# Attention maps of four chunks or fewer: one bank and one copy for prefix and whole chunks, with two PSUM banks in turn

## What is computed

```python
def block(args):                       # y_a and y_b: one block of 128 queries
    s = jnp.einsum('bqhd,bkhd->bhqk', qi, k).astype(jnp.float32) * scale
    ...                                # y_a adds log_cum[t] - log_cum[s]
    s = jnp.where(mask, s, NEG)        # causal, pad keys never seen
    p = jax.nn.softmax(s, axis=-1)
    return jnp.einsum('bhqk,bkhd->bqhd', p.astype(v.dtype), v)
...
p = jax.nn.softmax(jnp.concatenate([s, sink], axis=-1), axis=-1)[..., :-1]   # y_c
o = jnp.einsum('bnhgqk,bnkhd->bnqhgd', p.astype(v.dtype), vx)
...
branches = jnp.stack([y_a * silu(a_z), y_b * silu(b_z), y_c * silu(c_z)], axis=2)
merged = jnp.sum(sigmoid(gates) * einsum('blnw,nwd->blnd', branches, w_branch), axis=2)
return x + merged @ w_out
```

## Time and profile before

| what | value |
|---|---|
| median of 3 runs | 2737.91 us (2735.36 to 2740.32) |
| the profiled execution's own time | 2737.13 us |
| its span, first to last instruction | 2735.3 us |
| TensorE matmul (PE) busy | 2637.4 us, 96% |
| VectorE (DVE) busy | 1639.7 us, 60% |
| ScalarE (ACT) busy | 1136.1 us, 42% |

### The profile page before, as it was taken

How to read it: one execution, slowest core, us unless ns; L and a number is a source line. 1 busy time by engine, 2 the same in 40 slices (tenths; PEclk the granted TensorE clock), 3 DMA queues, 4 the chain that set the end, 5 groups by cost and what they waited for, 6 DMA issues and landing times. The chain is left out here.

```text
span 2735.3 us, 40191 instructions
## 1 busy us (share of the span) xinstructions
PE 2637.4 (96%) x15248; PEld 2188.7 (80%) x15248; DVE 1639.7 (60%) x3832; ACT 1136.1 (42%) x2518; POOL 129.5 (5%) x140
## 2 busy tenths in 40 slices
PE   8999999999999999999999899999998899999999
PEld 7879889899988777777877577888885658788887
DVE  5475666765547576675678663444567864533346
ACT  4345332543334543443435543333355664432333
POOL 1001000000100100000013000000004300000000
PEclk9999999999999999999999999999998999999999
DMA  4201212222220212222322122232321102323322
GB/s 136 79 30 55 67 42 84 58 74 89 86 80 27 76 58 59 81 66 93 99 81 62 32 89 93 95 98 93 94 90 46 42 1 78 91 95 95 98 96 97
DMA packets 115265, 205.30 MB, mean 75 GB/s; under 512 B 13824, under 2 KB 23680, under 8 KB 114944
## 3 DMA queue, kind: packets, MB, share of 16 engines
q1 hardware_dynamic: 114064, 200.14, 23.8%
q10 hardware_dynamic: 1008, 2.59, 0.3%
HBM read 200.51 MB, written 2.10 MB: 74 GB/s over the span
## 5 line engine op out<-in xcount | busy, mean ns | idle before, releaser
L1879 DVE TENSOR_TENSOR wl<-raw,wh 128x512 fp32r<-128x512 f32 (+2 forms) x738 | 481.3, 677 | 383.8 <-ACT wh L1678 374.4
L1678 ACT ACTIVATE wh<-raw 128x512 fp32r<-128x512 f32 (+2 forms) x774 | 450.6, 605 | 327.0 <-PE pp L2395 239.7
L2389 PE MATMUL pp<-Hh,wh 128*128 128x264 f32 (+1 forms) x2144 | 514.7, 355 | 11.1 <-ACT wh L1678 5.1
L2392 PE MATMUL pp<-Hl,wh 128*128 128x264 f32 (+1 forms) x2144 | 501.1, 348 | 0.0
L2395 PE MATMUL pp<-Hh,wl 128*128 128x264 f32 (+1 forms) x2144 | 499.6, 347 | 0.0
L2389 PEld LDWEIGHTS pp<-Hh,wh 128*128 128x128 f32 x2144 | 354.8, 190 | 71.4 <-issue 11.1
L2392 PEld LDWEIGHTS pp<-Hl,wh 128*128 128x128 f32 x2144 | 358.5, 190 | 51.7 <-issue 5.5
L2395 PEld LDWEIGHTS pp<-Hh,wl 128*128 128x128 f32 x2144 | 357.0, 190 | 51.3 <-issue 4.2
L2389 PE MATMUL pp<-Yh,wh 128*128 128x512 f32 (+1 forms) x1190 | 295.6, 364 | 1.9 <-ACT M L1743 0.7
L2392 PE MATMUL pp<-Yl,wh 128*128 128x512 f32 (+1 forms) x1190 | 289.6, 359 | 0.1
L2395 PE MATMUL pp<-Yh,wl 128*128 128x512 f32 (+1 forms) x1190 | 289.4, 359 | 0.1
(11 more groups left out here) (301 smaller groups left out, 3140.2 us busy)
## 6 DMA issues: line engine op xcount, KB each, us to landing
raw<-in_w SPq DMA_DIRECT2D x698, 256.0 KB, 2.6
raw<-in_w SPq DMA_DIRECT2D x36, 192.0 KB, 2.4
raw<-in_w SPq DMA_DIRECT2D x40, 128.0 KB, 2.0
out<-X SPq DMA_DIRECT2D x8, 256.0 KB, 2.0
con<-in_con SPq DMA_DIRECT2D x1, 1513.0 KB, 7.5
X<-in_x SPq DMA_DIRECT2D x2, 528.0 KB, 5.7
X<-in_x ACTq DMA_DIRECT2D x2, 528.0 KB, 6.6
Z<-in_p ACTq DMA_DIRECT2D x2, 512.0 KB, 3.6
```

What stands on the lines that cost most here:

```text
L1678: e.activation(part("wh", j), landing(j), AF.Copy).then_inc(*act.up("split", j))
L1879: e.tensor_tensor(part("wl", j), landing(j), part("wh", j).bitcast(F), ALU.subtract).then_inc(*dve.up("split", j))
L2389: done = e.matmul(it.ps, wh, xh, start=it.first and x == 0, stop=False)
L2392: done = e.matmul(it.ps, wh, xl, start=False, stop=False)
```

## The change

In `turn`, a map with fewer than four whole chunks puts its prefix chunk behind the whole ones, in the same bank and the same copy. `u["apart"]` keeps whether a prefix stayed apart, for the waits of the product. Where `divided` is set and no prefix is apart, units take bank 4 and bank 5 in turn (`tb`), by the parity of the unit's place in its attention. The blocks i = 3 of the four causal attentions of the first stack have four whole chunks and stay as they were.

```diff
             whole = [c for c in u["chunks"] if c[1] == 128]
             small = [c for c in u["chunks"] if c[1] != 128]
+            if len(whole) < 4:
+                whole, small = whole + small, []
+            u["apart"] = bool(small)
             n = u["n"]
             k = next(turns)
+            tb = 4 + k % 2 if divided and not small else 4
...
-            do("turn", ..., free5=free[5], free4=free[4], ..., b4=bank(4), b5=bank(5),
+            do("turn", ..., free5=free[5], free4=free[tb], ..., b4=bank(tb), b5=bank(5),
...
             if whole:
-                free[4] = (copier(u), "turned", n)
+                free[tb] = (copier(u), "turned", n)
...
-                maps.append(Item(..., small=any(x[1] != 128 for x in v["chunks"]), whole=any(x[1] == 128 for x in v["chunks"]),
+                maps.append(Item(..., small=v["apart"], whole=len(v["pt"]) > v["apart"],
```

More of the change, by code:

```diff
@@ L446, in left @@
                 return ("pe", "product", n - k + (k - ring) // each * each + each - 1) if k >= ring else None
-            do("turn", u=n, qr=qr, p=p, exp=u["exp"], small=small[0][0] if small else None, whole=[c[0] for c in whole], free5=free[5], free4=free[4],
-               pt_free=left(len(maps_at)), small_free=left(len(small_at)) if small else None, now=now, ident=ident, b4=bank(4), b5=bank(5),
+            do("turn", u=n, qr=qr, p=p, exp=u["exp"], small=small[0][0] if small else None, whole=[c[0] for c in whole], free5=free[5], free4=free[tb],
+               pt_free=left(len(maps_at)), small_free=left(len(small_at)) if small else None, now=now, ident=ident, b4=bank(tb), b5=bank(5),
                pt=pt, small_pt=low, by=copier(u))
@@ L477, in product @@
                 c, half = divmod(v["o"] // 64, 2)
-                maps.append(Item(u=v["n"], by=copier(v), pt=v["pt"], small=any(x[1] != 128 for x in v["chunks"]), whole=any(x[1] == 128 for x in v["chunks"]),
+                maps.append(Item(u=v["n"], by=copier(v), pt=v["pt"], small=v["apart"], whole=len(v["pt"]) > v["apart"],
                                  o=bank(bk)[64 * half:64 * half + 64, 128 * c:128 * c + 128] if halves else bank(bk)[0:v["qr"], v["o"]:v["o"] + v["dv"]]))
```

## The result

| | before | after |
|---|---|---|
| median (range, runs) | 2739.11 us (2735.36 to 2743.73, 4) | 2723.15 us (2719.75 to 2725.95, 4) |
| profiled execution, its span | 2737.13, 2735.3 us | 2724.57, 2722.8 us |

The ratio is 0.994 with a 95% interval of 0.992 to 0.9961: the change gains 0.6%, or 16 us by the medians and 12.6 us by the two profiled executions. The forecast was 2728, 10 to 11 us of gain: right in sign, in the main mechanism and in its range of 2719 to 2739, too small in size. Inside the narrower bracket (2723 to 2732) it fell by 0.15 us only, less than two executions differ by, and that much is luck.

A forecast was written before the change was run, and what follows sets the result against it. TensorE was taken as the bound, matmul side busy 2637.4 of 2735.3 us. Removed waits of 13.9 us, three quarters kept (10.4), plus 0.5 relief, less 1.0 added, gave -9.9 us: 2728 us, range 2719 to 2739.

The forecast's parts named there:

- Prefix transposes and bank 5: Blocks 0 to 2: prefix transposes no longer wait for the previous unit's prefix copy by VectorE; 5.7 to 10.1 us go.
- The even unit of block 2: Unit 30 takes bank 4, so its two waits for overflow readings in bank 5 go: 1.5 to 1.9 us.
- The copy of the unit before: Whole transposes no longer wait for the previous unit's copy, outside the differential attention: 3.1 to 5.5 us go.
- VectorE's relief: VectorE is relieved of 24 us beside TensorE's work; between 0 and 24 us of gain, 0.5 taken.
- relief counts: Rival: all removed waits stay gone and a fifth of VectorE's relief shows too: 18.7 us gained, 2719; chance 0.16.
- Three quarters kept: TensorE reaches VectorE's next results earlier and waits again; three quarters of the 13.9 us of removed waits are kept: 10.4.
- (a): Products wait for one wide copy instead of two copies, later by 0.107 to 0.133 us: 0 taken, 5.2 without cover.
- (b): Block 3's first overflow scores wait for ScalarE's four-chunk copy in bank 5: 0 to 2.5 us added, 1.0 taken.
- (c): An odd unit at the end of block 2 waits for an overflow reading in bank 5, as its prefix did: 0.
- Swallowed: Rival: stalls move to the next masking or division, a quarter kept: 2.5 us gained, 2735.5; 0.20 including no effect.
- late products: Rival: 40 product groups each wait a whole four-chunk copy, 24 us: 14 us slower, 2752; chance 0.08.
- Falling clock: Rival: TensorE granted 0.93 in the seven stretches loses about 45 us: 2773; sign, a clock under 0.99; chance 0.02.

The follow-up runs named there:

- E1: Changed kernel, but every unit transposes into bank 4; the prefix still shares the whole chunks' copy: 2728.71 us, ratio 0.9962 to the kernel before.
- E2: Changed kernel, but prefix chunks keep bank 5 and their own VectorE copy; units without a prefix alternate banks 4 and 5: 2729.8 us, ratio 0.9976 to before.
- E3: Changed kernel plus one unread 128x128 VectorE copy for each of the 112 merged units: 2723.76 us, ratio 0.9944 to the kernel before.
- E8: Changed kernel with each copy of transposed chunks in the seven attentions made twice: 2749.05 us, ratio 1.0029 to the kernel before.
- E5: Changed kernel, but the causal attentions' last units of block 2, near the first overflow scores, stay in bank 4: 2719.73 us, ratio 0.991 to before.
- E4: Changed kernel with two banks in turn also in the differential attention and the one over selected keys: 2722.1 us, ratio 0.994 to the kernel before.
- E6: E5 with two banks in turn also in the attention over selected keys, not the differential one: 2717.05 us, ratio 0.9904 to the kernel before.
- E7: E6 with the 32 remaining prefix copies, in blocks 3 of the causal attentions, made by ScalarE instead of VectorE: 2712.04 us, ratio 0.9888 to before.

## Why the prediction came out as it did

- *Prefix transposes and bank 5* (5.7 to 10.1): right. The row L2478 for L2133 went from 6.0 us to 0.3, as counted. E1, which has the shared copy alone, gains 10 us by its ratio, and 6.4 (3.1, 1.8 and 1.5) in the three causal attentions whose clock stayed at 1.00.
- *The even unit of block 2* (1.5 to 1.9): right; the row L2482 for L2119 fell by 1.5 in 2.
- *The copy of the unit before* (3.1 to 5.5): the term that was mis-sized. Its part alone (E2) gives 3.3 + 1.0 + 4.3 = 8.7 us in three attentions. I set aside the waits of the dilated attention as waits for divisions, by the name that the view gave; what they ended on was a copy. I was half right all the same: with the copy out of the way the division is waited for, and of 6.3 us of waits 3.3 are left.
- *VectorE's relief* (0.5): right to be small; E3 puts it at 0.3 us in all over the six attentions that can be compared. The rival "relief counts" gave a time closer to the result (2719) for a cause that E3 excludes.
- *Three quarters kept*: right in kind. In a of layer 0 the waits of PE show what came back; before (126.59 to 218.53 us), then after (127.53 to 216.88):

```profile
PE pp L2478 <- DVE plain L2133: 2.4, 5, 0.8
PE pp L2483 <- DVE P L2156: 1.5, 1, 1.5
...
PE pp L2478 <- DVE st L2115: 0.6, 1, 0.6
```
```profile
PE pp L2487 <- DVE P L2160: 2.4, 3, 1.5
...
PE pp L2482 <- DVE plain L2137: 0.3, 1, 0.3
```

  2.1 + 0.6 = 2.7 us of waits went, and two waits for divisions came beside the 1.5 of the first unit: 0.9 us. Two thirds were kept there, and about half in the dilated attention (3.0 of 6.3).
- *What is added*: (a) products cost nothing, as said; at twice the length of the copies (E8) it is 1.1 us. (b) overflow scores behind ScalarE's copies, 1.0 taken, cost 2.5 in three attentions by E5, already the upper end that I gave for four. The waits that E5 takes away are 1.3 us by the view, so about half of the 2.5 isn't seen as a wait there. (c), taken as nothing, is one new wait, at an odd unit of b in layer 0 (timeline of PE after):

```profile
369.92 0.30 PE L2487 MATMUL pp<-con,P 128*128 128x128 f32 x1 [0.38 <-DVE st L2119]
```

- *Swallowed, late products*: neither came.
- *Falling clock*: not at the size feared, but the sign that I had named, under 0.99 in these stretches, was there in two of seven (0.96 and 0.97). The same code was granted 1.00 in both in E4, so the change does not bring it by necessity. The Trainium skill (TensorE: Matmul & The Clock Gate, "A second HAM failure mode: psum-queue depth-cycling") tells of a kernel whose clock swung as it cycled through banks. E4, which cycles most, had 1.00 in all seven, and E1, which stays on one bank, 0.97 and 0.98 in two, so the runs do not bear it out here. Whether the change costs a little clock on average is open: the whole executions were granted 0.9870 in the mean of 34 of the kernel before, and 0.9861 in 29 of the changed kernel, E3, E4, E5, E6 and E7.

With both terms put right, the 9.9 us of the sum become some 12: the dilated attention gives 4.3 where three quarters of 0.7 to 1.1 stood (3.6 more), and (b) takes 1.5 more. The seven attentions gave 13.2 as profiled, and some 17 at an even clock (14.7, and 1.2 and 1.1 for b of layer 0 and the dilated one, by E4). So the bracket's middle or the kept share was still too low; which of them no run tells.

## What to carry to other kernels

- The name in a wait row is the latest count of an engine that was reached, not always the instruction waited for. Where the named instruction is one that nothing waits for, look in the timeline for the one just ahead of it in the queue that reports to the waiter. And what goes with it is only the time down to the next thing the waiter needs: 3.0 of 6.3 us here.
- A PSUM bank that is refilled each turn ties TensorE to the copying engine's queue; a second bank loosens this as far as the queue has room. 25 us of other copies put back cost nothing (E3), while the wide copies made twice, 59 us more of busy VectorE and 54 of ScalarE over the seven attentions, took the whole gain and more (E8). And a bank borrowed from another step brings that step's waits along (E4, E5; in the two a it made the second bank a loss until E5), so count its other users first.
- When stages differ by a few us, cut both traces at the same instructions and compare stage by stage with the granted clock beside each; the medians could not tell the changed kernel, E3 and E4 apart, nor E5 from E6.

## What the hardware showed that I had not expected

The granted clock alone moves identical stretches by more than most of these edits: b of layer 0, 131.91 us at 0.96 and 128.75 at 1.00; the dilated attention, 63.86 at 0.97 and 62.73 at 1.00. The work in each pair is the same, and so is what TensorE did before the clock fell. In the changed kernel it stood for 2.25 us in b of layer 0, waiting for a prefix copy (to 389.89), and from 392 to 395 it was granted 0.50, the 1.2 GHz level. E4 has the same wait, 2.3 us, and was granted 1.00 all through. What makes the clock fall in one execution and not in another I have not tested.

It is most of why executions of one kernel spread over 10 us and more. Sorted by the granted clock of the whole execution, the kernel before took (34 executions, run in turn with the experiments on two chips):

| granted clock | executions | time, us |
|---|---|---|
| 0.985 | 5 | 2742.86 to 2745.57 |
| 0.987 | 5 | 2736.78 to 2739.55 |
| 0.989 | 4 | 2733.1 to 2734.33 |

Over all 34 clock and time go together with a correlation of -0.97, and 0.001 of clock is worth about 2.5 us. The changed kernel's four executions took 2721.73 to 2725.95 us at 0.985 (three) and 2719.75 at 0.987: at the same clock it is 18 to 20 us faster than before, rather than the 16 of the medians. An estimate by a straight line through all executions of the ten kernels gives E1 and E2 8 to 9 us each at equal clock, and E3 and E4 17 to 18, the sum of the two. So E1's part and E2's are of one size, which their medians hide, and the forecast of 10 to 11 us was short by more than the medians say.
